# A four-layer decoder and a two-branch block on one core: opening and closing seams rewritten, the last projection beside attention changed, and one PSUM bank per head for turned probabilities and outputs

## The reference, cut to what matters

```python
for i in range(4):                       # kinds: mla, swa, fox, mla
    h = x @ w_in                         # queries, keys, values and a gate
    p = softmax(q @ k.T * scale + mask)  # per head, two blocks of 128 queries
    o = p @ v
    x = layernorm(ALPHA * x + (o * silu(gate)) @ w_out)
h = modulate(x, g, shift1, scale1)       # shift, scale, gate come from c @ w_ada
x = x + gate1 * ((g_pool * (pooled @ wp) + g_attn * (attn @ wa)) @ w_out)
h2 = modulate(x, g2, shift2, scale2)
q = h2 @ peer_wq                         # 1024 x 2048, the first product of PEER
x = x + gate2 * peer(h2)                 # 128 x 128 experts, all of them computed
return rmsnorm(x, g_final)
```

## Time and profile before

| | us |
|---|---|
| median of 3 timed runs | 1747.11 (1745.22 to 1751.63) |
| the profiled execution | 1730.18 |
| its span, first to last instruction | 1728.4 |
| PE busy | 1615.2 (93%) |
| DVE busy | 1180.4 (68%) |
| ACT busy | 865.2 (50%) |

### The profile page before, as it was taken

The page is one execution under the profiler, slowest core; times in us unless marked ns, Lnnn a source line. Parts: engine busy times, 40 slices in busy tenths (PEclk is TensorE's granted clock), DMA queues, the critical chain, the costliest instruction groups (busy, mean ns, idle before and its releaser), DMA issues.

```text
span 1728.4 us, 31280 instructions
## 1 busy us (share of the span) xinstructions
PE 1615.2 (93%) x10766; PEld 1392.1 (81%) x10766; DVE 1180.4 (68%) x2504; ACT 865.2 (50%) x1391; POOL 81.1 (5%) x110
## 2 busy tenths in 40 slices
PE   5889999998998889998999999899999999999996
PEld 4667877896677667776899999899999777778885
DVE  3565656755576666546347999788787999975554
ACT  3564544444556644453235666655655444445553
POOL 1030101100111210000000000000000000000000
PEclk9999989999998989999689999999999999999998
DMA  6544544555555447534244455544444454566552
GB/s 219 174 147 146 195 147 134 189 172 182 175 194 190 163 141 246 164 102 146 97 145 133 162 193 168 172 159 157 157 158 146 159 167 160 166 207 193 192 192 81
DMA packets 77188, 284.83 MB, mean 165 GB/s; under 512 B 9376, under 2 KB 9408, under 8 KB 75840
## 3 DMA queue, kind: packets, MB, share of 16 engines
q1 hardware_dynamic: 73296, 266.95, 46.5%
q0 software_dynamic: 3824, 16.99, 2.9%
HBM read 281.77 MB, written 2.14 MB: 164 GB/s over the span
## 4 chain that ended last, share of the span: by engine, by line
PE 74%; DVE 16%; ACT 4%; issue 3%; DMA 3%; DVEq 0%; SPq 0%; POOL 0%; ACTq 0%
PE banks L639 21%; PE banks L641 20%; PE banks L640 20%; DVE w_lo L1372 5%; PE banks L1027 3%; PE banks L774 2%; DMA raw<-stream 2%; PE banks L811 2%; PE banks L729 2%; PE banks L751 1%; DMA arena<-x_spill 1%; PE banks L823 1%; PE banks L822 1%; DVE arena L1841 1%; ACT w_hi L1085 1%
## 5 line engine op out<-in xcount | busy, mean ns | idle before, releaser
L1372 DVE TENSOR_TENSOR w_lo<-raw,w_hi 128x1024 fp32r<-128x1024 f32 x456 | 558.4, 1229 | 343.1 <-ACT w_hi L1085 338.5
L1085 ACT ACTIVATE w_hi<-raw 128x1024 fp32r<-128x1024 f32 x456 | 481.7, 1058 | 520.2 <-PE banks L641 478.5
L639 PE MATMUL banks<-w_hi,xT_hi 128*128 128x512 f32 (+1 forms) x1140 | 453.8, 398 | 14.9 <-DVE xT_lo L1406 6.0
L641 PE MATMUL banks<-w_hi,xT_lo 128*128 128x512 f32 (+1 forms) x1140 | 442.8, 388 | 0.0
L640 PE MATMUL banks<-w_lo,xT_hi 128*128 128x512 f32 (+1 forms) x1140 | 442.6, 388 | 0.0
L639 PE MATMUL banks<-xT_hi,w_hi 128*128 128x256 f32 (+1 forms) x1392 | 409.2, 294 | 4.9 <-DVE xT_lo L1406 2.9
L640 PE MATMUL banks<-xT_lo,w_hi 128*128 128x256 f32 (+1 forms) x1392 | 403.6, 290 | 0.0
L641 PE MATMUL banks<-xT_hi,w_lo 128*128 128x256 f32 (+1 forms) x1392 | 403.5, 290 | 0.0
L639 PEld LDWEIGHTS banks<-xT_hi,w_hi 128*128 128x128 f32 x1392 | 277.4, 199 | 6.0 <-DVE xT_lo L1406 3.1
L640 PEld LDWEIGHTS banks<-xT_lo,w_hi 128*128 128x128 f32 x1392 | 277.4, 199 | 0.1
L641 PEld LDWEIGHTS banks<-xT_hi,w_lo 128*128 128x128 f32 x1392 | 277.0, 199 | 0.0
(11 more groups left out here) (189 smaller groups left out, 1445.8 us busy)
## 6 DMA issues: line engine op xcount, KB each, us to landing
raw<-stream SPq DMA_DIRECT2D x504, 512.0 KB, 3.6
arena<-ln_in POOLq DMA_DIRECT2D x4, 1024.0 KB, 5.3
arena<-x_spill POOLq DMA_DIRECT2D x3, 1024.0 KB, 10.9
arena<-mod_rows POOLq DMA_DIRECT2D x2, 1536.0 KB, 9.7
arena<-g_in POOLq DMA_DIRECT2D x3, 512.0 KB, 10.6
arena<-x_in SPq DMA_DIRECT2D x2, 512.0 KB, 4.0
arena<-bands_in POOLq DMA_DIRECT2D x1, 1024.0 KB, 6.7
arena<-keys_in POOLq DMA_DIRECT2D x1, 1024.0 KB, 6.1
```

The costliest lines, as they stand in the source:

```text
L639: pe.matmul(out, stationary[0], moving[0], start=first, stop=False, **k)
L641: return pe.matmul(out, stationary[1], moving[0], start=False, stop=last, **k)
L1085: act.activation(w_hi[:, s], half_raw(s), ACT.Copy).then_inc(piece_hi, 1)
L1372: dve.tensor_tensor(w_lo[:, s], half_raw(s), w_hi[:, s].bitcast(F32), ALU.subtract).then_inc(piece_lo, 1)
```

## The change

Five places are edited. (1) The first units of all carry no wait on each other's banks, `open_first` turns both token blocks at once, and ACT and DVE take them out before they split weights. (2) The opening of PEER turns both blocks, waits for both, and projects all four feature units with `project`; on DVE the modulation of block 1 stands one piece earlier. (3) swa and fox: both gate units come among the first units; the unit beside attention is now the second half of the queries (swa) or of the values (fox), ACT takes it out after the exponentials of two heads, and the first `ada_chunk` moves to turn 3. The order of chunks in the stream follows (`CHUNK_ORDER`). (4) All attention loops: head g uses bank 6 + g % 2 for both its transposes and its outputs, transposes wait for the division of the head two before (`out_taken`), and DVE divides head i-3 in turn i. (5) The last four pieces run block 0 first, then block 1; the block's closing follows its own matmuls, with the root's table loaded before.

```diff
@@ Unit lists
-                    after = (earlier[half],) if earlier else (closing[0],) if closing else ()
+                    after = (earlier[half],) if earlier else (closing[0],) if closing else (None,)
...
-                L["gate"] = token_units(attn["gate"], D, SILU2, at=(0,))
+                L["gate"] = token_units(attn["gate"], D, SILU2)
+                L["kv"] = [Unit(plan, "mixed", [attn["kT"][:, 0:2], attn["v"][:, :, 0:256]], COPY2, pieces=4)]
                 L["q"] = feature_units(attn["qT"], KD, [("act", "scaled"), ("dve", "scaled")])
-                L["kv"] = [Unit(plan, "mixed", [attn["kT"][:, 0:2], attn["v"][:, :, 0:256]], COPY2, pieces=4)]
-                L["gate"] += token_units(attn["gate"], D, SILU2, at=(COLS,))
-                L["late"] = L["kv"] + L["gate"][1:]
+                L["late"] = L["q"]
...
@@ PE, attention
                     pe.wait_ge(probs_ready, g + 1)
-                    if g >= 1:
-                        pe.wait_ge(probsT_ready, g)
+                    if g >= 2:
+                        pe.wait_ge(out_taken, g - 1)
                     for c in range(3):
-                        mm = pe.transpose(banks[:, 6, c * P:(c + 1) * P], probs[:, g % 2, c * P:(c + 1) * P], ident)
+                        mm = pe.transpose(banks[:, 6 + g % 2, c * P:(c + 1) * P], probs[:, g % 2, c * P:(c + 1) * P], ident)
...
                     pe.wait_ge(probsT_ready, g + 1)
-                    if g >= 1:
-                        pe.wait_ge(out_taken, g)
-                    o = banks[:, 7, 0:2 * HD]
+                    o = banks[:, 6 + g % 2, 3 * P:3 * P + 2 * HD]
...
-                    if ada and i == 0:
+                    if ada and i == first_ada:
@@ PE, first opening and opening of PEER
-                turn_block(0)
-                project_opening(unit, turned, lambda: turn_block(1))
+                for b in range(B):
+                    turn_block(b)
+                project_opening(unit, turned)
...
-            open_layer(E["q"][0], E["hT"], h_half, 4, peer["h"])
-            for u in E["q"][1:]:
+            for n, u in enumerate(E["hT"]):
+                pe.wait_ge(h_half, 4 + n + 1)
+                turn(u, peer["h"])
+            wait_put(pe, E["hT"])
+            for u in E["q"]:
                 project(u)
@@ PE, the end
-            with pe.Fori(0, HALF // RING) as i:
+            with pe.Fori(0, HALF // RING - 1) as i:
                 for s in range(RING):
                     second_table(RING * i + HALF, s)
+            for b in range(B):
+                for s in range(RING):
...
+                    for d in range(D // COLS):
+                        mm = parts_product(banks[:, 2 * b + d], [x[:, s, b * P:(b + 1) * P] for x in (xT_hi, xT_lo)],
...
+                if b == 0:
+                    mm.then_inc(first_block, 1)
@@ ACT, attention
+                    if i == 1 and last is not None:
+                        evacuate_only(last)
...
-                        act.activation(probsT[:, g % 2], banks[:, 6, 0:384], ACT.Copy).then_inc(probsT_ready, 1)
+                        act.activation(probsT[:, g % 2], banks[:, 6 + g % 2, 0:384], ACT.Copy).then_inc(probsT_ready, 1)
@@ ACT and DVE, the first layer
-                    split_ahead(0)
                     for u in L["xT"]:
                         evacuate_only(u)
+                    split_ahead(0)
@@ DVE, attention
-                for i in range(2, heads + 2):
+                for i in range(2, heads + 3):
...
-                    if i >= 2:
-                        normalise(i - 2)
+                    if i >= 3:
+                        normalise(i - 3)
@@ DVE, opening of PEER
+            pieces_behind(out, 2)
+            modulate_block(peer["h"], moba["mod"][:, 4], moba["mod"][:, 3], 1)
             pieces_behind(out, 3)
-            modulate_block(peer["h"], moba["mod"][:, 4], moba["mod"][:, 3], 1)
-            pieces_behind(out, RING)
             for u in E["hT"][2:4]:
                 evacuate_only(u)
+            pieces_behind(out, RING)
@@ DVE, the end
+            dve.wait_ge(first_block, 1)
+            close_end(0)
+            norm_end(0)
+            dve.wait_ge(piece_used, n_pieces)
+            close_end(1)
+            norm_end(1)
```

More of the change, by code:

```diff
@@ L66 @@
 ADA_UNITS = 6 * D // COLS // DEPTH
+CHUNK_ORDER = dict(swa=((6, 10), (4, 6), (0, 4)), fox=((8, 10), (0, 8), (12, 16), (10, 12)))
 GATE_GROUPS = ((0, 4), (4, 8), (8, 12), (12, 15), (15, 16))
@@ L357, in build @@
                 L["k"] = feature_units(attn["kT"], KD)
+                L["gate"] = token_units(attn["gate"], D, SILU2)
                 L["v"] += token_units(attn["v"], D, at=(COLS,))
-                L["gate"] = token_units(attn["gate"], D, SILU2)
-                L["late"] = L["gate"]
+                L["late"] = L["gate"][1:] + L["v"][1:]
                 L["oT"] = split_turn_units(KD)
-            moved = {"mla": 0, "swa": 6, "fox": 8}[kind]
             L["chunks"] = (plan[-1].pieces_done - (layers[-1]["out"][-1].pieces_done if layers else 0)) // 2
-            L["order"] = [moved, moved + 1] * (moved > 0) + [n for n in range(L["chunks"]) if not moved or n not in (moved, moved + 1)]
+            L["order"] = [n for lo, hi in CHUNK_ORDER.get(kind, ((0, L["chunks"]),)) for n in range(lo, hi)]
             last = L["late"][1].pair
@@ L678, in block_products @@
                 x = [part[:, k, block * P:(block + 1) * P] for part in (xT_hi, xT_lo)]
-                if unit.kind == "token":
-                    return parts_product(bank[0][:, 0:unit.cols], x, [part[:, kt, 0:unit.cols] for part in w], first, last,
-                                         skip_group_check=True)
-                for t in range(4):
-                    at = (t % 2) * S + block * P
-                    mm = parts_product(bank[t // 2][:, at:at + P], [part[:, kt, t * P:(t + 1) * P] for part in w], x,
-                                       first and t % 2 == 0 and block == 0, last, skip_group_check=True)
-                return mm
+                return parts_product(bank[:, 0:unit.cols], x, [part[:, kt, 0:unit.cols] for part in w], first, last,
+                                     skip_group_check=True)
             def project_closing(units):
@@ L699, in project_closing, with project_opening @@
                         mm.then_inc(unit_full, 1)
-            def project_opening(unit, turned, turn_other):
+            def project_opening(unit, turned, turn_other=None):
                 bank_free(unit)
@@ L707, in project_opening @@
                             wait_put(pe, [turned[2 * b + n // 2]])
-                        if b == 0 and n == RING - 1:
+                        if b == 0 and n == RING - 1 and turn_other is not None:
                             turn_other()
                         w = take_piece(n if b == 0 else 0)
-                        bank = [bank_of(unit, b)] if unit.kind == "token" else [bank_of(unit, 0), bank_of(unit, 1)]
                         for kt in range(PK):
-                            mm = block_products(unit, b, bank, w, PK * n + kt, kt)
+                            mm = block_products(unit, b, bank_of(unit, b), w, PK * n + kt, kt)
                         if b:
@@ L800, in turn_gated, with attention @@
                 turn(layers[l]["oT"][half], o)
-            def attention(heads, q, k, v, ada=0, late=(), beside=(), gated=None):
+            def attention(heads, q, k, v, ada=0, late=(), beside=(), gated=None, first_ada=3):
                 g0 = heads_done[0]
@@ L900, in _ @@
                     attention(HEADS, queries, keys, lambda h, b: mla["kv"][:, b, 2 * HD * h + HD:2 * HD * (h + 1)],
-                              ada=ADA_CHUNKS, late=L["late"], gated=(l, mla["o"]))
+                              ada=ADA_CHUNKS, late=L["late"], gated=(l, mla["o"]), first_ada=0)
                     o = mla["o"]
                 elif L["kind"] == "swa":
-                    for u in L["q"] + L["kv"]:
+                    for u in L["gate"][1:] + L["kv"] + L["q"][:1]:
                         project(u)
-                    wait_put(pe, L["q"] + L["kv"])
+                    wait_put(pe, L["kv"] + L["q"][:1])
                     def half(h):
@@ L1134, in _, with attention @@
             heads_done = [0]
-            def attention(heads, kind, last_gate=None, mix=None, beside=()):
+            def attention(heads, kind, last=None, mix=None, beside=()):
                 g0 = heads_done[0]
@@ L1230, in _ @@
                     act.wait_ge(fox_loaded, 48)
-                    for u in L["gate"][:1] + L["q"] + L["kv"]:
+                    for u in L["gate"] + L["kv"] + L["q"][:1]:
                         evacuate(u)
-                    split_ahead(L["gate"][1].pieces_done - 1)
-                    evacuate_only(L["gate"][1])
+                    split_ahead(L["late"][1].pieces_done - 1)
                 else:
@@ L1240, in _ @@
                     act.activation(forget[:, 2], forget[:, 2], ACT.Ln, bias=1.0).then_inc(f_exp, 1)
```

(10 more changed lines are left out.)

59 lines of the change are left out of this document (34 added, 25 removed).

## The result

The changed kernel takes 1679.11 us (median of 4 runs, 1667.24 to 1683.77), the kernel before 1746.16 in the same measurement (4 runs): a ratio of 0.960, with a 95% interval from 0.954 to 0.966. Predicted were 1691.6 (1675 to 1710). Later runs give 1675.33 for the changed kernel (6 runs) and 1742.9 for the one before (57 runs in all). The ratios leave out the few executions that lie more than 1.5% above the fastest of their kernel (3 of these 57), so a ratio and two medians can say slightly different things. So the gain is 67 us, and the sum said 55.5. The two profiled executions differ by only 46.4 (1730.18 and 1683.77).

The account below looks back on a forecast made before the run. PE was taken as the bound, busy 1615.2 of 1728.4 us. Four terms, 10.7 + 23.5 + 6.3 + 15 = 55.5 us, off a timed 1747.1 gave 1691.6 us, with a range from 1675 to 1710.

Parts of the forecast that it names:

- Term 1: First opening: turning both blocks at once removes PE's 11.88 us wait for `xT_lo`; gain 10.7 us, bounds 8.1 and 12.2.
- rival 5: First opening held by weights: piece 4 late by 3 us, time 1695, inside the main case; no separate chance given.
- Term 2: Opening of PEER: 192 narrow matmuls become one more unit of 96; gain 23.5 us, bounds 19.5 and 27.
- rival 3: PEER's clock stays down: its four units run at 0.50, 43 us lost, time 1735; chance 0.03.
- Term 3: The end: block 0 closes while PE runs block 1's matmuls; gain 6.3 us, bounds 5.5 and 6.7.
- Term 4: Attention, three parts: start in swa, start in fox, the other turns; gain 15 us, bounds -4 and 23.
- The starts in swa and fox: First two parts of Term 4: new unit order gains 4 us in swa (0 to 6), 4.4 in fox (1 to 7).
- The other turns: Third part of Term 4: shorter turns from the new banks, 6.6 of 10.2 us waits; bounds -5 and 10.2.
- Rival 1: Attention: bank hand-off eats its gain; time 1698, or 1706.6 if the starts give nothing either; chance of either 0.12.
- Rival 2: Attention in swa and fox keeps its clock, up to 7 and 4 us shorter; time 1680; chance 0.08.
- Rival 4: Slower: in attention, transposes wait for the division in every turn, 72 heads pay; 1764 at 1.0 us each; chance 0.02.
- The offset of 16.9 us: Whole kernel: timed median above the profiled execution of 1730.18 us, assumed the same before and after the change.

## Why the prediction held, and where its sum was off

**Term 1, right.** 10.7 was predicted; 11.5 in the profiles, 13.5 by medians, 9.4 by the ratio. The weights did not hold the unit (rival 5): what still holds its start is DVE's first split, 2.98 us at 13.07.

**Term 2, right in size, and its reason was tested.** 23.5 predicted, 23.8 in the profiles, 24.5 timed. PE starts 11.3 us after the first transposes where it started 4.2 us after them, as worked out. The clock came up (rival 3 is out). The Trainium skill ("TensorE: Matmul & The Clock Gate", Part 1) says that the half clock is the default and activity releases it. Here PE's row is as busy in the 192 narrow matmuls (40.70 of 41.00 us), and the clock stayed down in all of them.

**Term 3, right.** 6.3 predicted, 6.3 in each of eight profiles; alone, the timed runs can't tell it from nothing. Of this 6.2 stand ahead of the end of the last scaling and 0.1 behind it, where I had put 6.0 and 0.3.

**Term 4 is the one that was mis-sized, in two of its three parts.**
- *The starts in swa and fox*: 4 and 4.4 were predicted, 18.3 timed for that edit alone (11 to 24 by its interval), and 10.4 is the difference of the profiles. The step that failed is "415.8 + 12.3 + 2 = 430.1" set against 434.48: it took one execution's fox layer for the rule. In that profile head 4's transposes come 111.0 us after the transposes of block 1 at the layer's opening; in five other profiles of the same unit order they come 118.2 to 119.2 after them, where PE then runs at half clock for 24 to 34 us and not for the 6.8 that I saw (a sixth has 111.2). One of the five:

```profile
419.00:449.00 30.00, 29.33 (x107) 17.92 (x103) 9.68 (x30) 9.58 (x32) 1.26 (x1) 0.51 0.32 108
```

With the new order it is 105.0 to 111.6 in seven. In swa the same execution was a long one, 74.5 against 70.5 to 70.8 in four of the others. What shows in every profile is this: the first transposes of attention come 2.9 us sooner after the opening in swa and 8 to 11 in fox, where the chunk and its DMA wait of 4 to 5 us stood ahead of them; part of it is given back in turn 3, where the chunk now stands. PE also spends less time at half clock in the two layers: 20 to 65 us in the profiles without the new order (38 on average) and 7 to 44 with it (26). By an estimate from this, 12 us less at half clock save 6 us; the spread is too wide to call it shown.
- *The other turns*: 6.6 predicted, 6.1 timed, with an interval from 0 to 10.6. The size fits and the place is wrong. I spread it over four layers at 1.5 each. It is 4.0 and 5.4 in the two mla layers, and in swa and fox no gain shows: the wait for the division that I put in turn 3 is there in swa (1.60), and in fox the DMA's stall covers it. "None elsewhere" was wrong: the last two turns of every layer wait 0.55 to 1.14 us each for it. PE's waits for ACT in attention came to 1.5 us (the exponential), under the 5 that I had said; the 7.0 for the division come on top.

**Rival 1 is out in mla.** The Trainium skill ("PSUM — Partial Sum Buffer", section on bank collisions) allows no two engines in the same partitions of one bank at once, and I worked out a gain of 0 from the hand-off that follows. The hand-offs are there, as waits of 0.55 us in the last turns, and the layer is still 3.4 us or more shorter in each of seven profiles, since they replace longer ones (1.06 and 0.85 us in the kernel before). From the first to the last head's transposes the first mla layer takes 30.8 us in all seven and 32.6 without the edit. Just behind them PE's clock is at 0.50 for 3 to 10 us in each of the seven profiles without it and in none with it.

**Rival 2** (attention keeps its clock), given 0.08, names the time nearest to the measured one, 1680, though its own terms (5.5 and 3.6 off 1691.6) give 1682.5. Its mechanism isn't what happened: the clock still falls in swa and fox in every profile, in stretches of 3 to 31 us.

**Rival 4 is out.** The transposes wait for the division in 9 places and not in all 72 turns.

**The offset of 16.9 us was no constant.** I carried it over as if it were part of measuring. It was the clock of one execution. Over the 57 runs of before the time goes from 1728.5 at a mean granted clock of 0.964 up to 1759.2 at 0.943, about 1.5 us for each 0.001, and the line through them gives 1731 at the 0.961 of the profiled one. It lies 12.7 us under their median, and its fox layer alone is 9 to 16 us shorter than in five of the six other profiles without the new order (171.3 against 180.3 to 186.8). So the offset and the error in term 4 are one mistake, made twice: an execution whose fox layer was fast was taken for the usual one. The profile of the changed kernel (0.968) lies 8 above that of its ten runs, 1675.5. These two explain why 46.4 us between the profiles are 67 between the medians.

**Luck.** That the time came out within the range, 12.5 us under the forecast, is in part luck: the range was wide enough for a term 4 of 24 to 31 us instead of 15. By the medians the parts add up to 13.5 + 24.5 + 3.4 + 6.1 + 18.3 = 65.8, by the ratios to 59.6, each part uncertain by 5 to 8 us. So they agree with the 65 to 70 of the whole as far as such medians can tell.

**What stays open.** Why PE's clock falls for 3 us in one profile of a kernel's attention and for 30 in the next. Neither the new banks (old banks, 30.7 us) nor the chunk's DMA wait (without it, 30.7 in swa) is needed for it. That the new unit order makes the long falls rarer is what the timed runs suggest; in the fox layer they are 24 us or longer in five of seven profiles without it and in one of seven with it (two more have 20.5), and no run isolates the cause.

## What to carry to other kernels

Look at the clock in the windows before taking a stretch of one profile for its usual length; where a stage starts from a stall, get a second profile, or set the timed runs' clocks against the profiled one's. A wait that is seen in the profile and a wait put in its place can both be read off; what a stage costs after them, at half clock, is the larger and the less certain part. And where tokens are split for the sake of an early start, count matmuls: here, at half clock, each half cost as much as the whole.

## What the runs showed of the hardware

- **At 1.2 GHz an fp32r matmul of 128 columns is no shorter than one of 256.** In the last rows shown above the starts of 256-column matmuls are 0.21 us apart at half clock (892.53, 892.74), and 192 of 128 columns take 41.0 us there, 0.21 each. No run shows the narrow ones at full clock. If the same holds there, an estimate is that the 192 would take the time of two units of 96, 23 us, instead of 11.5.
- **A fully busy PE stayed at 1.2 GHz for 47 us** (831.6 to 878.7 in the kernel before). Every profile with the narrow opening (six) has the clock at 0.50 from its start to its end, in a stretch of 48 to 51 us, and it is back at 1.00 3 to 5 us into the 256-column unit behind.
- **The time of one kernel on one chip varies with the granted clock**: the changed one by 0.7%, 1667.5 at 0.978 to 1678.8 at 0.972 in six runs, the one before by 1.5%, 1732.8 at 0.962 to 1758.5 at 0.942 in 17 runs. The two profiles of the changed kernel, 9 us apart, have the same instructions and the same waits for the division.
